# Moving the final norm of a decoder trunk behind the drains of its token tiles, and splitting the last V rows between TensorE and VectorE

## What is computed

```python
def rmsnorm(x, g):
    return x * lax.rsqrt(jnp.mean(x * x, axis=-1, keepdims=True) + EPS) * g

# each token: 8 heads, 16 picks a head, so 128 picks
a = jnp.einsum('cd,ckd->ck', hx, u_tab[e])
out = jnp.einsum('ck,ckd->cd', g * jax.nn.gelu(a), v_tab[e])
...
x = x + peer_ffn(h2, ...)          # last step of each layer
return rmsnorm(x, final_g)         # after the second layer
```

## Time and profile before

| | us |
|---|---|
| median of 3 runs (3820.3 to 3822.63) | 3821.1 |
| the profiled execution | 3815.32 |
| its span, first to last instruction | 3813.5 |
| PE / DVE / POOL / ACT busy in the span | 3223.0 / 2537.4 / 2348.9 / 944.4 |
| mean granted TensorE clock, share of 2.4 GHz | 0.914 |

### The profile page before, as it was taken

How to read it: one execution, slowest core, us unless ns; L and a number is a source line. 1 busy time by engine, 2 the same in 40 slices (tenths; PEclk the granted TensorE clock), 3 DMA queues, 4 the chain that set the end, 5 groups by cost and what they waited for, 6 DMA issues and landing times.

```text
span 3813.5 us, 37766 instructions
## 1 busy us (share of the span) xinstructions
PE 3223.0 (85%) x11488; PEld 2088.0 (55%) x11488; DVE 2537.4 (67%) x6141; ACT 944.4 (25%) x2087; POOL 2348.9 (62%) x2114
## 2 busy tenths in 40 slices
PE   7889889978997989967988999877988976767676
PEld 6778756545674656535765656544765632323223
DVE  6545397876656788876566888776566887444443
ACT  3220234223211234332211333322211322111111
POOL 1100266767666766766666776767667777777773
PEclk9789999979998999979999999988999998888888
DMA  4324599999999999999999999999999999999995
GB/s 155 138 100 168 201 389 364 380 362 363 390 401 375 399 359 385 378 356 350 386 403 364 408 367 380 383 356 354 390 393 370 390 346 334 372 372 355 375 362 221
DMA packets 361577, 1305.56 MB, mean 342 GB/s; under 512 B 40417, under 2 KB 42849, under 8 KB 361121
## 3 DMA queue, kind: packets, MB, share of 16 engines
q0 software_dynamic: 298960, 1087.79, 75.1%
q1 hardware_dynamic: 62416, 215.35, 14.8%
HBM read 1288.30 MB, written 14.68 MB: 342 GB/s over the span
## 4 chain that ended last, share of the span: by engine, by line
PE 35%; POOL 24%; DMA 17%; issue 12%; DVE 11%; ACT 1%; another core or an unknown queue 1%; DVEq 0%; ACTq 0%; POOLq 0%
POOL heap L877 24%; DMA heap<-table_u,heap 17%; PE ps L916 14%; PE ps L1119 13%; DVE heap L2051 3%; PE ps L964 2%; DVE heap L1754 2%; PE ps L1059 1%; PE ps L1043 1%; DVE hT L1873 1%; PE ps L1003 1%; PE ps L1009 0%; PE ps L1072 0%; PE ps L1021 0%
## 5 line engine op out<-in xcount | busy, mean ns | idle before, releaser
L1119 PE MATMUL ps<-heap 128*128 128x512 f32 x3260 | 1634.4, 640 | 368.0 <-ACT heap L1371 238.7
L2051 DVE CUSTOM_DVE_ANT_0 heap<-heap 128x1024 f32<-128x1024 f32 x1024 | 1252.2, 1223 | 942.0 <-DMA heap<-table_u,heap 874.2
L877 POOL DMA_INDIRECT heap<-table_v,heap x1024 | 1189.4, 1162 | 686.9 <-issue 262.5
L877 POOL DMA_INDIRECT heap<-table_u,heap x1024 | 1125.0, 1099 | 341.0 <-issue 311.4
L1119 PEld LDWEIGHTS ps<-heap 128*128 128x128 f32 x3260 | 646.9, 204 | 1057.0 <-issue 747.6
L916 PE MATMUL ps<-hT,ring 128*128 128x256 f32 x3840 | 893.5, 383 | 19.0 <-DVE hT L1873 12.7
L916 PEld LDWEIGHTS ps<-hT,ring 128*128 128x128 f32 x3840 | 735.1, 192 | 225.6 <-issue 135.9
L1371 ACT ACTIVATE heap<-ident,heap 128x128 f32<-128x128 f32 x815 | 293.1, 392 | 524.7 <-DVE heap L2062 301.4
L1391 ACT ACTIVATE heap<-heap 128x8 f32<-128x8 f32 x128 | 26.7, 209 | 1018.8 <-DVE heap L2051 809.0
L1754 DVE SCALAR_TENSOR_TENSOR heap<-heap 128x1024 f32<-128x1024 f32 x203 | 260.4, 1283 | 10.5 <-DVE stats L1920 4.5
L848 POOL DMA_DIRECT2D ssm_par<-heap x8 | 4.5, 566 | 283.9 <-DVEq L1616 283.9
(11 more groups left out here) (247 smaller groups left out, 2607.4 us busy)
## 6 DMA issues: line engine op xcount, KB each, us to landing
ring<-weights SPq DMA_DIRECT2D x344, 512.0 KB
ring<-ssm_par SPq DMA_DIRECT2D x48, 512.0 KB
heap<-table_u,heap POOLq DMA_INDIRECT x1024
heap<-table_v,heap POOLq DMA_INDIRECT x1024
ssm_par<-heap POOLq DMA_DIRECT2D x20, 512.0 KB, 6.6
ring<-weights SPq DMA_DIRECT2D x20, 256.0 KB
xT<-x_cm SPq DMA_DIRECT2D x2, 1024.0 KB, 9.4
ssm_par<-heap POOLq DMA_DIRECT2D x8, 256.0 KB, 2.8
```

What stands on the lines that cost most here:

```text
L877: pool.indirect_dma_start(rows[:, j, :], None, table, bass.IndirectOffsetOnAxis(expert[:, tile % 2, k:k + 1], 0)).then_inc(landed, 16)
L1119: mm = pe.matmul(ps[:, 4 + 2 * (tile % 2) + half, :], diag[:, PE_TURN[v] % DIAGS, :], rows_v[:, v % NV, half * 512:(half + 1) * 512], star ...
L2051: dve.tensor_tensor_reduce(row, row, h_tok[:, tile % 2, :], 1.0, 0.0, ALU.mult, ALU.add, act_st[:, g % 3, pick % GROUP:pick % GROUP + 1]). ...
```

## The change

The final norm becomes an item of the plan (`final`, with parts on ACT, PE, ACT and DVE). It is taken in three pieces (`FINALS`: the tile whose drain it waits for, first token, number of tokens): 256 tokens behind the drain of tile 5, 128 behind that of tile 6, 128 behind that of tile 7. The first also waits for the last transposition of `hT` (`htok`), the others for the piece before. The loops behind the list are gone; SP stores each piece as it is ready, the pieces of 128 tokens in runs of 512 bytes. A piece's squares wait for the stores of the pieces before it. PE writes the mean into bank 0, 1 or 2. Besides, the condition at L443 lets odd V rows go to DVE when no other work is left, from the 24th last row on: rows 1001 to 1021, eleven of them.

```diff
+    "final": ("ACT", "PE", "ACT", "DVE"),
+FINALS = ((TILES - 3, 0, N), (TILES - 2, N, P), (TILES - 1, N + P, P))
...
 # weight_of: PE (8, .4), ACT (4, .6) for the squares and (1, .6) for the root, DVE (9, .5)
 # prior:
+    if kind == "final":
+        return [end("htok", STAGES - 1, 1, 1)] + ([end("final", u - 1)] if u else [])
...
 # make_plan:
+    finals = deque(range(len(FINALS)))
-    while at < len(order) or v < TILES * PICKS or any(queue.values()) or shut:
+    while at < len(order) or v < TILES * PICKS or any(queue.values()) or shut or finals:
...
-            slot["v_on"] = "DVE" if ... and not queue["TOP"] and at < len(order) and (...) else "PE"
+            slot["v_on"] = "DVE" if ... and not queue["TOP"] and (at < len(order) or v >= TILES * PICKS - 24) and (...) else "PE"
...
+        while finals and ready([(("drain", FINALS[finals[0]][0]), 2)] + prior(("final", finals[0])), s):
+            enqueue(("final", finals.popleft()), 0, s)
 # run_sp:
-            for half in range(2):
-                sp.wait_ge(final_ready, half + 1)
-                sp.dma_start(out_cm[:, half, :].rearrange("p (k t) -> p k t", t=N), hT[:]).then_inc(out_stored, 16)
-            sp.wait_ge(out_stored, 32)
+            for n, (_, t0, width) in enumerate(FINALS):
+                sp.wait_ge(final_ready, n + 1)
+                sp.dma_start(out_cm[:, t0 // N, :].rearrange("p (k t) -> p k t", t=N)[:, :, t0 % N:t0 % N + width],
+                             hT[:, :, t0 % N:t0 % N + width]).then_inc(out_stored, 16)
+            sp.wait_ge(out_stored, 16 * len(FINALS))
 # run_pe:
+                if kind == "final":
+                    t0, width = FINALS[u][1] % N, FINALS[u][2]
+                    pe.wait_ge(bank_free[u], len([n for n in UNIT.values() if n % 4 == u]))
+                    pe.wait_ge(squares_done, 4 * (2 * STAGES + u + 1))
+                    for k in range(KD):
+                        mm = pe.matmul(ps[:, u, 0:width], mean_ones[:], hT[:, k, t0:t0 + width], start=(k == 0), stop=(k == KD - 1))
+                        if k == KD - 1:
+                            mm.then_inc(final_mean, 1)
+                        yield
+                    return
 # run_act:
+                elif kind == "final":
+                    tile, t0, width = FINALS[u]
+                    if part == 0:
+                        act.wait_ge(x_home, 2 * (tile + 1))
+                        if u == 0:
+                            act.wait_ge(tiles_done, len(RING_UNITS))
+                        else:
+                            act.wait_ge(out_stored, 16 * u)
+                        for i in range(4):
+                            act.activation(hT[:, 2 * i:2 * i + 2, t0 % N:t0 % N + width], xT[:, 2 * i:2 * i + 2, t0:t0 + width],
+                                           ACT.Square).then_inc(squares_done, 1)
+                            yield
+                    else:
+                        act.wait_ge(final_mean, u + 1)
+                        act.wait_ge(normed, 9 * (2 * STAGES + u))
+                        act.activation(rms[:, 0:width], ps[:, u, 0:width], ACT.Sqrt, bias=eps[:, 0:1]).then_inc(root_done, 1)
+                        yield
 # run_dve, with scale() now taking t0 and width:
+                elif kind == "final":
+                    _, t0, width = FINALS[u]
+                    yield from scale(t0, width, 2 * STAGES + u, fing)
+                    dve.wait_ge(normed, 9 * (2 * STAGES + u + 1))
+                    dve.sem_inc(final_ready, 1)
...
 # run_pe, run_act, run_dve: the loops "for half in range(2)" behind the list are removed
```

More of the change, by code:

```diff
@@ L169 @@
     "settle": ("DVE", "ACT"), "angles": ("DVE", "ACT"), "masks": ("PE", "DVE"), "pa": ("DVE", "ACT"), "pb": ("DVE",), "pd": ("DVE",), "ptb": ("DVE",), "pca": ("DVE",),
-    "ptab": ("DVE",), "tb": ("PE", "ACT"), "wt": ("PE", "ACT", "DVE"), "drain": ("DVE", "PE", "DVE"), "store": ("DVE",),
+    "ptab": ("DVE",), "tb": ("PE", "ACT"), "wt": ("PE", "ACT", "DVE"), "drain": ("DVE", "PE", "DVE"),
+    "final": ("ACT", "PE", "ACT", "DVE"),
 }
+FINALS = ((TILES - 3, 0, N), (TILES - 2, N, P), (TILES - 1, N + P, P))
 RINGED = ("mean", "ssm_u", "ssm_x", "ssm_y", "q", "k", "v", "att_s", "att_p", "att_o", "pool_u", "mix", "glu_gate", "glu_val",
@@ L184, in weight_of @@
                 "branch": (8 if item[-1] < 2 else 4, .43) if kind == "branch" else 0, "score": (4, .28), "htok": (4, .2),
-                "tb": (4, .2), "wt": (16, .28), "masks": (2, .3), "drain": (8, .2)}.get(kind, (16, .43))
+                "tb": (4, .2), "wt": (16, .28), "masks": (2, .3), "drain": (8, .2), "final": (8, .4)}.get(kind, (16, .43))
     if eng == "ACT":
-        return {"squares": (4, .6), "mean": (1, .5), "ssm_u": (16, .29), "ssm_y": (16, .29), "q": (4, .6), "k": (4, .6),
+        return {"squares": (4, .6), "final": (4 if part == 0 else 1, .6), "mean": (1, .5), "ssm_u": (16, .29), "ssm_y": (16, .29), "q": (4, .6), "k": (4, .6),
                 "att_e": (1, .25 + .0011 * att_blocks(item[2]) * P) if kind == "att_e" else 0, "att_o": (1, .3), "mix": (2, .4),
@@ L193, in weight_of @@
             "pb": (44, .2), "pd": (8, .6), "ptb": (18, .55), "pca": (24, .55), "ptab": (75, .3), "wt": (4, .29),
-            "drain": (2, .7)}.get(kind, (1, .3))
+            "drain": (2, .7), "final": (9, .5)}.get(kind, (1, .3))
 def final_part(kind):
@@ L442, in make_plan @@
             slot["v"] = v
-            slot["v_on"] = "DVE" if v % PICKS % 2 == 1 and v % PICKS < PICKS - 1 and not queue["TOP"] and at < len(order) and (v < PICKS or ready([(("drain", v // PICKS - 1), 1)], s)) else "PE"
+            slot["v_on"] = "DVE" if v % PICKS % 2 == 1 and v % PICKS < PICKS - 1 and not queue["TOP"] and (at < len(order) or v >= TILES * PICKS - 24) and (v < PICKS or ready([(("drain", v // PICKS - 1), 1)], s)) else "PE"
         busy = slot["u"] is not None or slot["v"] is not None
@@ L726, in trunk @@
         x_home = sem("x_home")
+        final_mean = sem("final_mean")
         final_ready = sem("final_ready")
@@ L1136, in run_pe @@
             assert not live
[L1137 to L1141, removed]
         def run_act(act):
@@ L1392, in run_act @@
             assert not live
[L1393 to L1402, removed]
         def run_dve(dve):
@@ L1864, in settle, with scale @@
                 yield
-            def scale(u, n, gain, dst):
-                t0 = N * (u % 2)
+            def scale(t0, width, n, gain):
                 dve.wait_ge(root_done, n + 1)
-                dve.reciprocal(rstd[:], rms[:]).then_inc(normed, 1)
+                dve.reciprocal(rstd[:, 0:width], rms[:, 0:width]).then_inc(normed, 1)
                 yield
@@ L1872, in scale @@
                 for k in range(KD):
-                    dve.scalar_tensor_tensor(dst[:, k, :], xT[:, k, t0:t0 + N], gain[:, k:k + 1], rstd[:], ALU.mult,
-                                             ALU.mult).then_inc(normed, 1)
+                    dve.scalar_tensor_tensor(hT[:, k, t0 % N:t0 % N + width], xT[:, k, t0:t0 + width], gain[:, k:k + 1],
+                                             rstd[:, 0:width], ALU.mult, ALU.mult).then_inc(normed, 1)
                     yield
@@ L1882, in emit @@
                     at = V_G2 if item[2] else V_G1
-                    yield from scale(u, NORMS[item], vec[:, u // 2, at:at + KD], hT)
+                    yield from scale(N * (u % 2), N, NORMS[item], vec[:, u // 2, at:at + KD])
+                elif kind == "final":
[3 more added lines that the diff above has]
+                    dve.sem_inc(final_ready, 1)
                 elif kind == "ssm_x":
@@ L2085, in run_dve @@
             assert not live and not pending
[L2086 to L2092, removed]
         with nc.Block() as block:
```

## The result

The changed kernel takes 3799.8 us (median of 8 runs, 3787.0 to 3808.4) against 3827.6 us for the kernel before (8 runs, 3820.3 to 3832.2). The ratio is 0.9935, its 95% interval 0.9918 to 0.9952: 18 to 31 us less, where 19.9 were forecast. The profiled execution took 3799.67 us, its span 3797.9, 15.6 us under the span of before.

What follows compares the result with a forecast made beforehand. Transfers were taken to pace the gathers, then an uncovered chain after the last dot. The terms -18.7 - 6.7 + 2.5 + 3.0 = -19.9, from a median of 3821.1, gave 3801.2 us; 8-in-10 range 3794 to 3810.

Steps and rivals of the forecast that it cites:

- Step a: Behind the last drain: only a 128-token norm stays, 10.7 us instead of 29.4, so -18.7 us (-21.1 to -13.7).
- Step b: After the last dot: DVE takes five V rows, PE six; sums end at 3773.6 instead of 3780.3, -6.7 us.
- the -1.3 worked out from it for the rows: Last row sums: if PE stays at the lower clock for all six rows, they save only 1.3 us.
- Step c: Among the gathers: moved norms cost +2.5 us on DVE and +3.0 us for stores, nothing for new waits.
- The part for DVE: First moved norm, during the last top-k sorts: half of its 5.0 us of DVE work is paid, +2.5 us.
- The part for the stores: Gather stage: 1.57 MB of stores displace gathered bytes at 368 GB/s, near the full price of 4.3 us, +3.0 us.
- The new waits: Gather stage: waits on ACT and PE for the norms cost nothing, at most one POOL wait of 7.2 us.
- The prediction's own sign here: End of the gathers: the last dot comes some 5 us later than 3756.5 us.
- rival 2: Gather stage: moved norms are free, stores fill holes and DVE work lies in waits; -25.4, 3795.7 us; chance 0.13.
- 1, PE at 1.2 GHz to the end: After the last dot: rows and mean run at the lower clock throughout; -13.1, 3808.0 us; chance 0.13.
- 3 and 4, stalls: Gather stage: one 7.2 us POOL stall, 3808.4 us, chance 0.11; or seven hand-offs starving gathers, 3851.6 us, chance 0.03.
- 5, the norms come too late to matter: Later norms become possible only near the end, so only the rows move; about 3814 us; chance 0.03.

Runs made afterwards that it cites:

- e4: Changed kernel with the final norm in two pieces of 256 tokens instead of three, the second behind the last drain; ratio 0.9966 to the kernel before.
- e3: Changed kernel with 12 unread matmuls of 128 columns on PE between the last drain's transposes and the last mean; ratio 0.9937 to the kernel before.
- e6: Changed kernel with 32 more scalings of 128x256 on DVE in the first norm, results unused; ratio 0.9921 to the kernel before.
- e5: Changed kernel with the first piece's 1 MB store issued seven times more, to a spare tensor; ratio 0.9972 to the kernel before.
- e7: Changed kernel with odd V rows on DVE from the 12th last row on instead of the 24th last; ratio 0.9946 to the kernel before.
- e1: Changed kernel without the new V rows on DVE, only the norm in three pieces; ratio 0.9945 to the kernel before.
- e9: Changed kernel with the last six V rows gathered into the free U buffers; ratio 0.9922 to the kernel before.

## Why the prediction was right

**Step a, the norm behind the last drain: right, 1.6 us too good.** It was to go from 29.4 to 10.7 us; it went to 12.35 (3785.55 to 3797.9), -17.1 for -18.7. Piece by piece: squares 1.33 (taken 1.25), root 0.37 (0.36), reciprocal 0.95 (0.9), scalings 2.19 (2.2), store 3.72 from the last scaling's end (3.6), hand-offs 0.30 (0.35), the table load hidden as argued. The one term that was off is the mean: 3.49 us, over its upper bound of 2.7, where 2.0 was taken because "PE will have idled only some 3 us". It had idled 2.83, and was granted 0.55. Rows at hand spoke against the choice: half of 3.62 us at 1.00 is 1.8 us at the higher level, and twice that, 3.6, at the lower. The bound was half of the 5.44 us mean of before, which had not been slow all through: the clock was 0.50 in its first 2 us and 0.78 over the rest, and the last mean of e4, as wide, took 6.39 us. e3 shows the cause: 2.05 us when PE was given work. The sum's upper bound of 15.7 is also too low: the upper bounds of its terms add to 16.4.

**Step b, the last rows: right, 1.5 us too good.** The sums end 17.4 us after the last dot, predicted 16 (-5.2 for -6.7). Five rows on DVE and six on PE came, the first two slow (0.50, then 0.77 while the clock rises), three rows in 8.04 us where 8.3 were taken. The gathers were mis-sized: 1020's was to be issued 4.0 us after the last dot and used 5.2 us later; it was issued after 4.7 (3769.05, when row 1014 was done) and used after 6.0 (3775.08); 1022's took 6.2 (3771.86 to 3778.09). The 5.2 us were one row's time, from a gather of U. The wait that replaced the one removed was named rightly: the gathers of the last rows.

At the rows the clock came back, as the trace of before had it: two rows slow, the rest at 1.00. At the mean it fell, behind 2.83 us of idle. By the Trainium skill, TensorE: Matmul & The Clock Gate, "What's actually happening", throttled is the default and activity releases it; the trace agrees at the mean, where the prediction had not applied it, and not with the -1.3 worked out from it for the rows.

**Step c, what the moved norms cost inside: too much, as far as it can be told.** +5.5 was forecast. From the htok copy to the last dot the ten profiles with norms inside have a mean of 683.3 us, the three without 682.3: +1, in a spread of some 6 either way. The timed runs say the same: 18 to 31 us saved in all, 22.3 of them at the end, leaves between 9 gained and 4 lost for the rest, and 5.5 lost lies just outside. The part for DVE, +2.5, has no support in e6: five times as much work cost nothing to be seen. The part for the stores, +3.0, isn't shown either: e5 gives 2.4 to 3.5 us for each of seven stores more, in a stage that they fill, but the change's own store went into that stage without fewer gathers. The 337 GB/s that was held against rival 2 may have been the room for it. The new waits starved nothing that the profiles show.

The prediction's own sign here, the last dot some 5 us later than 3756.5, seems to have come true (3763.2), but 11.1 us of the delay arose ahead of the htok copy; counted from there, the last dot came 4.4 us earlier, which is its sign for rival 2.

**The rivals.** 1, PE at 1.2 GHz to the end: not for the rows, though 1.4 us of its price of 6.8, the slow mean, came true. 2, free inside: the nearest to what was measured inside, where nothing is seen; its 25.4 us for the end missed the same 3.1 us as the forecast. 3 and 4, stalls: one wait of POOL for PE of 7.2 and 9.3 us does occur with the norms inside (e7, e1), at 3160 us, some 70 us behind the htok copy. Before had its 7.2 at 3168 us, with no norm inside, so such a wait needs no hand-off of a norm. 5, the norms come too late to matter: they stand at 3088 and 3447 us. (The 700 and 340 us that the prediction gives for the times of the earlier trace rows are 739 and 378 us before the end.)

**The number.** 3801.2 was forecast, 3799.8 measured. That it is so close is luck: the end came out 3.1 us worse than its two terms, the inside some 4 better, and the median of before beside it was 3827.6 where the forecast started from 3821.1. The interval of the ratio holds both the forecast's -19.9 (0.9948) and the -22.3 of the trace's end.

## What to carry to other kernels

Work that waits at the end for the last of its inputs should be cut so that only the last input's share is left there; what is moved among other work is paid for, if at all, on the resource that paces that stage (here seven stores more cost some 2.9 us each, while 13.4 us of work on a busy DVE cost nothing that could be seen). In a chain behind the last input, look at what each engine did in the microseconds ahead of its step: here a matmul group on a TensorE that was just idle took 1.7 times as long (3.49 us against 2.05), and twelve unread matmuls ahead of it bought that back. Compare two traces between points they share, so that a difference that arose elsewhere is not put down to the change.

## What was not expected of the hardware

- 2.83 us without a matmul, right behind a stretch at 1.00, and the next 16 records ran at a granted 0.55: 3.49 us against 2.05. The clock was still 1.00 when they began, and fell in their first 1.7 us.
- Two executions of one kernel reach the same point of the program 10 us apart (3074.4 and 3084.7 us at the last htok copy), while the end repeats within 0.5 us. What makes the difference was not settled.
- Behind the last dot, gathered V rows still took 6.0 to 6.2 us from issue to use (1020 and 1022 in the changed kernel, 1022 in e9), with the transfer engines 0.77 to 0.93 busy there, 0.96 in e9. In e9 no such gather waited for a buffer, and it was as long.
